# Sums of squares as one stacked product each, rope before the RMS scale, in the first mixer of a four-layer block

## What is computed

```
def rms_norm(x, gain):
    y = xf * lax.rsqrt(jnp.mean(xf * xf, axis=-1, keepdims=True) + EPS)
    return (y * gain.astype(jnp.float32)).astype(x.dtype)
...
    qkv = (h @ w_qkv).reshape(B, S, 3, N_GROUPS, A_HEADS, A_HEAD_DIM)
    for g, (window, dil) in enumerate(DIL_CONFIGS):
        q = rope(rms_norm(qkv[:, :, 0, g], q_gain[g]), S)
        k = rope(rms_norm(qkv[:, :, 1, g], k_gain[g]), S)
        v = qkv[:, :, 2, g]
        o, lse = dilated_group(q, k, v, window, dil)
```

## Time and profile before

| | before |
|---|---|
| device time, median of 3 runs | 2909.85 us (2908.01 to 2910.32) |
| profiled execution: its own time | 2913.05 us |
| its span, first to last instruction | 2911.2 us |
| TensorE busy | 2871.5 us (99%) |
| ScalarE / VectorE / GpSimd busy | 1619.1 / 1097.7 / 408.2 us |
| mean granted TensorE clock | 0.998 |
| DMA, both weight queues | 499.12 MB, 171 GB/s |

### The profile page before, as it was taken

How to read it: one execution, slowest core, us unless ns; L and a number is a source line. 1 busy time by engine, 2 the same in 40 slices (tenths; PEclk the granted TensorE clock), 3 DMA queues, 4 the chain that set the end, 5 groups by cost and what they waited for, 6 DMA issues and landing times.

```text
span 2911.2 us, 35690 instructions
## 1 busy us (share of the span) xinstructions
PE 2871.5 (99%) x13350; PEld 2380.6 (82%) x13350; DVE 1097.7 (38%) x2238; ACT 1619.1 (56%) x2413; POOL 408.2 (14%) x472
## 2 busy tenths in 40 slices
PE   9999999999999999999999999999999999999999
PEld 7989889888886778888887887888877788788887
DVE  6554736211214654111225114523244611642235
ACT  7675767544445765444456545545455644655455
POOL 1111111111111001111110111111111011111110
PEclk9999999999999999999999999999999999999999
DMA  8676767788887328888885797888878489788884
GB/s 247 152 160 137 177 135 161 166 192 193 193 192 161 75 56 201 195 194 195 192 194 118 153 194 165 197 192 196 185 179 189 90 183 194 168 188 190 200 193 116
DMA packets 137005, 499.12 MB, mean 171 GB/s; under 512 B 15344, under 2 KB 15600, under 8 KB 136720
## 3 DMA queue, kind: packets, MB, share of 16 engines
q0 software_dynamic: 67296, 245.59, 47.8%
q1 hardware_dynamic: 68688, 249.59, 27.6%
q10 hardware_dynamic: 864, 1.78, 0.2%
HBM read 494.81 MB, written 2.10 MB: 171 GB/s over the span
## 4 chain that ended last, share of the span: by engine, by line
PE 94%; ACT 2%; DVE 2%; issue 1%; DVEq 1%; DMA 0%; ACTq 0%
PE ps L1152 76%; PE ps L1171 5%; PE ps L1516 3%; PE ps L1271 1%; PE ps L1457 1%; PE ps L1436 1%; PE ps L1663 1%; ACT arena L1023 1%; PE ps L1641 1%; PE ps L1232 0%; PE ps L1372 0%; PE ps L1254 0%; PE ps L1446 0%; DVE XT L2243 0%; PE ps L1229 0%
## 5 line engine op out<-in xcount | busy, mean ns | idle before, releaser
L476 ACT ACTIVATE wh<-raw 128x1024 fp32r<-128x1024 f32 (+1 forms) x465 | 489.7, 1053 | 934.1 <-PE ps L1152 901.5
L1152 PE MATMUL ps<-HH,wh 128*128 128x512 f32 x2224 | 870.6, 391 | 3.9 <-DVE HL L2251 2.1
L1152 PE MATMUL ps<-HH,wl 128*128 128x512 f32 x2224 | 865.8, 389 | 0.0
L1152 PE MATMUL ps<-HL,wh 128*128 128x512 f32 x2224 | 865.6, 389 | 0.0
L460 POOL DMA_DIRECT2D wl<-weights x465 | 406.3, 874 | 2467.7 <-ACT wl L480 2467.5
L1152 PEld LDWEIGHTS ps<-HH,wh 128*128 128x128 f32 x2224 | 417.5, 188 | 95.9 <-issue 6.3
L1152 PEld LDWEIGHTS ps<-HL,wh 128*128 128x128 f32 x2224 | 417.6, 188 | 87.4 <-issue 1.4
L1152 PEld LDWEIGHTS ps<-HH,wl 128*128 128x128 f32 x2224 | 417.4, 188 | 87.2
L480 ACT ACTIVATE wl<-raw 128x1024 fp32r<-128x1024 f32 (+1 forms) x465 | 483.7, 1040 | 0.0
L1152 PE MATMUL ps<-MH,wh 128*128 128x512 f32 x1056 | 411.9, 390 | 2.0 <-issue 1.3
L1152 PE MATMUL ps<-MH,wl 128*128 128x512 f32 x1056 | 410.9, 389 | 0.0
(11 more groups left out here) (324 smaller groups left out, 3014.5 us busy)
## 6 DMA issues: line engine op xcount, KB each, us to landing
raw<-weights SPq DMA_DIRECT2D x468, 512.0 KB, 6.1
wl<-weights POOLq DMA_DIRECT2D x465, 512.0 KB, 7.8
XT<-x SPq DMA_DIRECT2D x4, 512.0 KB, 8.2
out<-XT SPq DMA_DIRECT2D x3, 512.0 KB, 2.7
arena<-tables POOLq DMA_DIRECT2D x1, 1024.0 KB, 11.2
arena<-table_h ACTq DMA_DIRECT2D x1, 640.0 KB, 6.3
arena<-swaps_a POOLq DMA_DIRECT2D x1, 576.0 KB, 8.4
out<-XT SPq DMA_DIRECT2D x2, 256.0 KB, 2.4
```

The lines of the kernel that those rows point to most:

```text
L476: act_f(wh[:, n, 0:w], raw[:, n, 0:w], ACT.Copy)
L1152: op = mm(bank(g, t), w[:, slot, at:at + P], x[:, first + kt, :], start=(kt == 0 and w is wh and x is xh), stop=(kt == n_k - 1 and w is wl ...
```

## The change

For each set of four tiles:
- The squares of a tile's upper and lower 64 rows are written to the same 64 rows (`a_squares`, two tiles an instruction), and VectorE adds them (`a_join`). What is left has 64 rows a tile.
- ScalarE writes the high part of that in 64 rows of a stack (`a_square_high`), and VectorE the low part in the other 64 (`a_lows`), so that one product of ones sums both: four products a set in place of eight. They stand all four behind kt 4.
- The copy to `qk` and the exponential are one instruction for the set; all factors come together, behind two slabs.
- The slab of `a_results` stands behind everything of the four tiles.
- VectorE makes the rope with the gain alone (`a_rope`), as soon as the copy is there, and multiplies the factor last (`a_scaled`). The factor is taken in the order of residues where the tile lies in it.

```diff
...
@@ -228,7 +228,7 @@
...
         sq = tiles3(7, NSQ)
-        sq_hi, sq_lo = MH[:, 6:8, :], ML[:, 6:8, :]
+        sq_stack = (MH[:, 6:8, :], ML[:, 6:8, :])
         rs = tiles3(11, 4)
...
@@ -388,6 +389,19 @@
...
             return bank(g, 2 + hd)
+        def stacked_rows(first):
+            rows = slice(0, 64) if first == 0 else slice(64, P)
+            return rows, slice(64, P) if first == 0 else slice(0, 64)
+        def by_residue(x):
+            return x.rearrange("p (l r) -> p r l", r=4)
+        def in_residues(x):
+            return x.rearrange("p (r l) -> p r l", r=4)
...
@@ -563,13 +577,16 @@
...
                 high_parts(s + (SLOTS + 2), 1)
+                k = c.take("join", 4)
                 act.wait_ge(q_first, 2)
-                a_squares(n, lambda t: qk[:, t, :], 0)
+                a_squares(qk[:, 0:2, :], 0)
+                a_square_high(k, 0)
                 high_parts(s + (SLOTS + 3), 1)
...
                 act.wait_ge(q_first, 4)
-                a_squares(n, lambda t: qk[:, t, :], 2)
+                a_squares(qk[:, 2:4, :], 2)
+                a_square_high(k, 2)
                 new_high(6)
...
@@ -609,43 +626,49 @@
...
-            def a_squares(n, tiles_in, first):
-                for t in (first, first + 1):
-                    add_waits(act, sq_used, n, t - 1)
-                    act_f(sq[:, t, :], tiles_in(t), ACT.Square)
-                    act_f(sq_hi[:, t % 2, :], tiles_in(t), ACT.Square).then_inc(sq_ready, 1)
-            def a_copies(g, tset, first):
-                for t in (first, first + 1):
-                    act_f(qk[:, 4 * tset + t, :], bank(g, t), ACT.Copy).then_inc(qk_kept, 1)
+            def a_squares(src, first):
+                rows, _ = stacked_rows(first)
+                act_f(sq[rows, 0:2, :], src[0:64], ACT.Square)
+                act_f(sq[rows, 2:4, :], src[64:P], ACT.Square).then_inc(sq_ready, 2)
+            def a_square_high(n, first):
+                rows, _ = stacked_rows(first)
+                act.wait_ge(sq_joined, (n + first).div(2).value(1))
+                act_f(sq_stack[first // 2][rows, :, :], sq[rows, 0:2, :], ACT.Copy).then_inc(sq_high, 1)
             def a_results(g, tset, last, between):
-                n = c.take("sq", 4)
+                n, k = c.take("sq", 4), c.take("join", 4)
                 wait_used(act, last)
-                a_squares(n, lambda t: bank(g, t), 0)
-                a_copies(g, tset, 0)
+                b = 4 * g.mod(2)
+                a_squares(ps[:, b:b + 2, :], 0)
+                a_squares(ps[:, b + 2:b + 4, :], 2)
+                act_f(qk[:, 4 * tset:4 * tset + 4, :], ps[:, b:b + 4, :], ACT.Copy).then_inc(qk_kept, 4)
+                a_square_high(k, 0)
+                a_square_high(k, 2)
                 between()
-                a_squares(n, lambda t: bank(g, t), 2)
-                a_copies(g, tset, 2)
                 return n
-            def a_rms(g, n, q, first):
-                for t in (first, first + 1):
-                    act.wait_ge(sq_used, (n + t).value(1))
-                    act.wait_ge(qk_done, (q + t).value(1))
-                    act_f(rs[:, t, :], bank(g, t), ACT.Ln, scale=1.0 / P, bias=cst[:, C_EPS6:C_EPS6 + 1])\
-                        .then_inc(acc_free[g.mod(2)], 1)
+            def a_rms(g, n, q, tset):
+                act.wait_ge(sq_used, (n + 3).value(1))
+                act.wait_ge(qk_done, (q + 3).value(1))
+                for t in range(4):
+                    src, dst = bank(g, t), rs[:, t, :]
+                    if (4 * tset + t) % 3:
+                        src, dst = by_residue(src), in_residues(dst)
+                    act_f(dst, src, ACT.Ln, scale=1.0 / P, bias=cst[:, C_EPS6:C_EPS6 + 1]).then_inc(acc_free[g.mod(2)], 1)
                 act.drain()
-                for t in (first, first + 1):
-                    act_f(rs[:, t, :], rs[:, t, :], ACT.Exp, scale=-0.5).then_inc(rs_ready, 1)
-            def a_next(g, n, q):
+                act_f(rs[:, :, :], rs[:, :, :], ACT.Exp, scale=-0.5).then_inc(rs_ready, 4)
+            def a_next(g, n, q, tset):
                 here, s = c.take("group"), c.take("slab", 4)
-                high_parts(s + SLOTS, 1)
-                a_rms(g, n, q, 0)
-                high_parts(s + (SLOTS + 1), 1)
-                a_rms(g, n, q, 2)
+                high_parts(s + SLOTS, 2)
+                a_rms(g, n, q, tset)
                 high_parts(s + (SLOTS + 2), 1)
...
@@ -1204,14 +1227,13 @@
...
-                if kt not in (1, 3):
+                if kt != 4:
                     return
-                for t in (kt - 1, kt):
-                    if k:
-                        pe.wait_ge(qk_kept, 4 * k + t - 3)
-                    pe.wait_ge(sq_low, 4 * k + t + 1)
-                    mm(bank(g, t), ones_r[:, :], sq_hi[:, t % 2, :], start=True, stop=False)
-                    mm(bank(g, t), ones_r[:, :], sq_lo[:, t % 2, :], start=False, stop=True).then_inc(sq_used, 1)
+                if k:
+                    pe.wait_ge(qk_kept, 4 * k)
+                for t in range(4):
+                    pe.wait_ge(sq_low, 2 * k + t // 2 + 1)
+                    mm(bank(g, t), ones_r[:, :], sq_stack[t // 2][:, t % 2, :], start=True, stop=True).then_inc(sq_used, 1)
...
@@ -1714,10 +1736,19 @@
...
-            def a_lows(n, first):
-                for t in (first, first + 1):
-                    dve.wait_ge(sq_ready, (n + t).value(1))
-                    v.tensor_tensor(sq_lo[:, t % 2, :], sq[:, t, :], sq_hi[:, t % 2, :], ALU.subtract).then_inc(sq_low, 1)
+            def a_join(n, first):
+                rows, _ = stacked_rows(first)
+                dve.wait_ge(sq_ready, (n + first).value(2))
+                v.tensor_tensor(sq[rows, 0:2, :], sq[rows, 0:2, :], sq[rows, 2:4, :], ALU.add).then_inc(sq_joined, 1)
+            def a_lows(k, first):
+                rows, other = stacked_rows(first)
+                dve.wait_ge(sq_high, (k + first).div(2).value(1))
+                dve.drain()
+                v.tensor_tensor(sq_stack[first // 2][other, :, :], sq[rows, 0:2, :], sq_stack[first // 2][rows, :, :],
+                                ALU.subtract).then_inc(sq_low, 1)
...
@@ -1763,10 +1794,12 @@
...
                     v.tensor_tensor(qk[:, t, :], bank(g, t), rs_first, ALU.mult).then_inc(q_first, 1)
-                lows = c.at["sq"]
-                a_lows(lows, 0)
+                squares, joined = c.at["sq"], c.at["join"]
+                a_join(squares, 0)
+                a_lows(joined, 0)
                 split(2, scaled(4), hf, parts(HH, HL, 4))
-                a_lows(lows, 2)
+                a_join(squares, 2)
+                a_lows(joined, 2)
                 split(2, scaled(6), hf, parts(HH, HL, 6))
...
@@ -1836,26 +1869,32 @@
...
-            def a_tile(hd_tile, n):
+            def a_rope(hd_tile):
...
                 gain = P_AQK + 3 * is_k + g3
+                def turned(out, rows, table):
+                    v.scalar_tensor_tensor(out=out, in0=x[rows, :], scalar=par[rows, gain:gain + 1], in1=tab[rows, table, :],
+                                           op0=ALU.mult, op1=ALU.mult)
+                low, high = slice(0, 64), slice(64, P)
+                dve.drain()
+                turned(t1, slice(0, P), 0)
+                turned(t2[low, :], high, 1)
+                turned(t2[high, :], low, 1)
+                dve.drain()
+                if g3 == 0:
+                    v.tensor_tensor(x, t1, t2, ALU.add)
+                else:
+                    v.tensor_tensor(in_residues(x), by_residue(t1), by_residue(t2), ALU.add)
+            def a_scaled(hd_tile, n):
                 dve.wait_ge(rs_ready, n.value(1))
-                v.scalar_tensor_tensor(out=xg, in0=x, scalar=par[:, gain:gain + 1], in1=rs[:, n.mod(4), :],
-                                       op0=ALU.mult, op1=ALU.mult)
-                dve.drain()
-                v.tensor_tensor(t1, xg, tab[:, 0, :], ALU.mult)
-                v.tensor_tensor(t2[0:64, :], xg[64:P, :], tab[64:P, 1, :], ALU.mult)
-                v.tensor_tensor(t2[64:P, :], xg[0:64, :], tab[0:64, 1, :], ALU.mult)
-                dve.drain()
-                if g3 == 0:
-                    op = v.tensor_tensor(x, t1, t2, ALU.add)
-                else:
-                    by = lambda y: y.rearrange("p (l r) -> p r l", r=4)
-                    op = v.tensor_tensor(x.rearrange("p (r l) -> p r l", r=4), by(t1), by(t2), ALU.add)
-                op.then_inc(qk_done, 1)
+                x = qk[:, hd_tile, :]
+                v.tensor_tensor(x, x, rs[:, n.mod(4), :], ALU.mult).then_inc(qk_done, 1)
...
@@ -1915,20 +1954,28 @@
...
                 g = gs + 1
-                n = c.take("sq", 12)
-                if pair:
-                    a_lows(n, 0)
-                    a_lows(n, 2)
-                for t in range(11):
-                    if t in (3, 7):
-                        a_lows(n + (t + 1), 0)
-                    a_tile(t, q + t)
```

(56 more changed lines are left out.)

## The result

| | before | changed |
|---|---|---|
| median, with the four runs of each | 2910.09 us (2908.01 to 2910.54) | 2943.68 us (2934.02 to 2951.19) |
| ratio, 95% interval | | 1.0116 (1.0098 to 1.0133) |
| profiled execution, its own time | 2913.05 us | 2934.02 us |
| its span | 2911.2 us | 2932.2 us |
| mean granted clock | 0.998 | 0.994 |

A forecast was written before the change was run, and what follows sets the result against it. TensorE, busy 99% of the span, was taken as the bound. Terms -11.0 - 1.0 + 11.4 + 6.7 = +6.1 us gave 2919.2 against the profiled execution, 2916 against the median; range 2904 to 2926.

The forecast's parts named there:

- Products: TensorE, 12 sets: four products of ones fewer in each, at 0.228 or 0.235 us apiece, 11.0 us off.
- The fourth slab: Eleven sets: slab 3's second transfer issued at 9.9, landing 8.2 later, TensorE waiting 1.1 or 0.5 us each; 11.4 us added.
- Pair 0: First set's longer ScalarE and VectorE chain: TensorE loses 0.7, 2.2 for the sums and 3.8 for slab 8; 6.7 us added.
- the input tiles: Pair 0's first set: the split of input tiles 4 and 5 ends later behind the low part, 0.7 us lost.
- VectorE, 20 us in a set of 23, costs nothing: VectorE's joins, low parts, ropes and factors fit in a set, with 2 us of cover for the low parts; no cost.
- rival 5: Clock falls to half behind the slab 8 wait in pair 0: 1.5 us, up to twice that, 2917 to 2919; chance 0.22.
- the 3.8 us of slab 8: Pair 0, first slab of `g2`: lands at 62.2 while TensorE wants it at 58.4, 3.8 us lost.
- the old wait in pair 0: Kernel before, first sums of pair 0: TensorE's wait for VectorE, counted as won, 1.0 us off.
- Rival 4: Transfers of the fourth slabs land at 9.1: 21 us in place of 11.4, pair 0 1 more, 2926; chance 0.1.
- Rival 2: The cover holds: no fourth slab is late, only 2.9 us of pair 0 stays, -9.1 us, 2901; chance 0.15.

The follow-up runs named there:

- Run 4: Changed kernel with the results' slab ahead of the high parts, and pair 0's first set done as in the kernel before: 2899.99 us, ratio 0.9971.
- run 1: Changed kernel with the slab of a set's results moved behind the copy, ahead of the two high parts: 2907.11 us, ratio 0.9993.
- run 3: Kernel before, with only the slab of a set's results moved behind all four tiles: 2933.41 us, ratio 1.0080.
- run 7: The changed kernel timed once more, nothing altered, beside the others on one chip: 2940.90 us, ratio 1.0109.
- run 2: Changed kernel with every product of ones done three times, 96 products more: 2933.23 us, ratio 1.0084.
- run 5: Changed kernel with a useless 1.8 us ScalarE copy between slab 3 and the next slab, except behind pair 0's first set: 2922.24 us, ratio 1.0043.
- run 6: Changed kernel with only pair 0's first set done as in the kernel before, the late slab kept: 2933.41 us, ratio 1.0086.

## Why the prediction was wrong

By its own steps:

- *Products*, -11.0: right in kind and size. Run 4 has 44 fewer (10.1 us), 1.2 us more of waits, and 8.8 us less.
- *The fourth slab*, +11.4: the mechanism is shown (runs 1 and 3), and this is **the term that was mis-sized**. The issue was priced at 9.9 on the set's clock and came at 10.55 (103.81 less 93.26): the squares of 64 x 1024 take 1.03 to 1.05 start to start and the high parts 1.07, not 0.95. The 0.1 us by which an instruction of ScalarE outlasts the distance to the next was taken off them too, and it is not there for these: the squares are 1.02 long. The landing was priced at 8.2 from transfers with one neighbour behind them; here two stand behind (1.8 and 3.7 us), and the median is 8.9. Together 1.35 us a set. The waits come to 17.2 us in the profiled execution and 20.5 in run 7's, without the restarts, in place of 11.4.
- *Pair 0*, +6.7: the chain came out as written, 1.9 for the sums and 2.9 for slab 8, with 0.3 and 0.7 for slabs 5 and 6, which TensorE reaches sooner when the first sums are gone. The second of these stands where 0.7 was forecast for the input tiles; run 7 has 1.0 for VectorE there (line 1734). Missed was what it did to the next set: VectorE finished the first set's factors at 70.4, when ScalarE had been done with squares and copy of the next set since 68.4, and a join takes 1.2 more; so slab 11 was 3.3 us later still, and TensorE waited 3.3 for it (part of the 17.2). The step "VectorE, 20 us in a set of 23, costs nothing" holds for a set in the middle and fails where the set before it began late.
- *The clock*, rival 5, is **the step that failed**. The sum had nothing for it, and rival 5 gave it 0.22, one place and 1.5 to 3 us, because a fall in the trace of before stood behind 4.7 us of idleness and only the 3.8 us of slab 8 seemed near that. The other fall in that trace stood behind 4.6 us, and the clock was at half for 6.8 us there. The rest of its waits are 1.5 us at most, so it could not tell what a wait between 1.5 and 4.6 us does. TensorE before, at 961.92:

```profile
961.92 0.79 PE L1372 MATMUL ps<-HH,wh 128*128 128x512 f32 x1 [4.58 <-ACT arena L779]
```

In the changed kernel it fell behind waits of 1.6, 1.9, 2.3, 2.9 and 3.3 us, and did not behind others of 1.7, 1.9, 2.3 and 2.6. The two executions of the change have five and nine spells in the mixer, at 1.6 us each: 8 to 14 us. Runs 2 and 5 shorten the waits, and two spells are left in each; run 4 has no wait above 0.7 us and no spell. By the Trainium skill (TensorE: Matmul & The Clock Gate, Part 1: The HAM clock gate) a spell of idleness closes the gate. The trace agrees with that much; the page has it for longer idleness than these waits, and the 1.6 us before 112.68, with the clock at half from 113.5 on, decide otherwise.

The balance for the mixer of the profiled execution: products -11.0, the old wait in pair 0 -1.0, fourth slabs 17.2, pair 0's other waits 6.5, the overlap that each of these 17 waits breaks, 0.16 apiece (2.7), five spells of 1.6 (8.0): +22.4. The next product behind a wait also starts 0.11 us late (0.24 in the set of values), 2.2 over the 17: +24.6 against the measured +24.2. Both faults carry the miss: of the 18 us above the forecast's +6.1, the clock has 8.0 and the fourth slabs with their restarts some 9; in run 7's execution, whose mixer is 32.8 us longer than before, they have 14.4 and some 12. What the other runs of the change have above the profiled one (median 9.7 us) can't be read from traces that weren't kept; run 7's trace has it as spells and as waits for VectorE.

Rival 4, late landings, was the nearest in time (2926). It had the right term at nearly the right size, in part by luck: its landings of 9.1 make up for an issue that was priced 0.65 us too early. What it lacks is the clock. Rival 2, the cover holds, is what run 1 brings about by moving the slab.

## What to carry to other kernels

When work on an engine is fused, look at what else stands in that engine's list behind it: here one weight slab behind the fused block, 8.1 us into its set where the kernel before has it at 2.9, cost three times what the saved products gave. With the same fused work and the slab at 6.0 us the 33 us are gone (run 6 against run 4), and no fourth slab is waited for (run 1). Put what the busiest engine waits for first, and what only feeds slack last; and price a wait on TensorE with its clock, which here took 1.6 us more behind several waits of 1.6 to 3.3 us. A trace that has no wait of the length you forecast cannot tell what the clock does behind it.

## What was not expected of the hardware

- Work added to ScalarE, 1.8 us in each of eleven sets, took 18.7 us off the change (run 5), and 96 products added to TensorE took 8 to 10 us off the change (run 2).
- The same second transfer of 512 KB lands in 8.0 us (median) with the next ones 3.7 us behind it and in 8.9 with the next ones 1.9 us behind; in run 3, also with the next slab directly behind, it was 9.3. By the DMA page of the Trainium skill (DMA: Bandwidth & Descriptors, section Queues, rings and completion order) the engines take turns between queues, by which `raw` transfers, which SyncE issues on the other queue, slow a second transfer that runs beside them; the medians agree with that. No run moves the `raw` transfers alone, so whether they or the next second transfers cost the 0.9 us is not shown. Why single ones land in 7.0 to 7.3 at the same spacing stays open.
- The clock fell to half for 3.4 us behind some waits of 1.6 to 3.3 us and not behind others as long. What tells them apart was not settled.
